# Gate/up norms: eight square tiles folded to two on GpSimd, their sum on TensorE one tile later, and the factor spread inside the fourth tile

## The chip, the cores and the metric

One NeuronCore of a Trainium2 chip runs the whole program. The metric is device time in microseconds (us), the median of several runs. One execution was also taken by the hardware profiler; all rows below come from it. Engine names are those of the profile: PE is TensorE (PEld its weight loads), DVE is VectorE, ACT is ScalarE, POOL is GpSimd, SP is the engine that issues the transfers.

## The reference

Two layers of an encoder over 576 positions (512 of a prompt and 64 of a sample), model width 1024, feed-forward width 2816. Each layer begins and ends with a half-step feed-forward block, so there are four of them:

```python
def rmsnorm(x, g):
    xf = x.astype(jnp.float32)
    y = xf * lax.rsqrt(jnp.mean(xf * xf, axis=-1, keepdims=True) + EPS)
    return (y * g.astype(jnp.float32)).astype(x.dtype)

def ffn_half(x, g, wg, wu, wd):
    h = rmsnorm(x, g)
    return x + 0.5 * ((jax.nn.silu(h @ wg) * (h @ wu)) @ wd)

def layer(h, ...):
    h = ffn_half(h, n1, w1g, w1u, w1d)
    z = rmsnorm(h, nm) @ w_in
    m, st = token_mix(z, ...)
    h = h + m @ w_out
    h = ffn_half(h, n2, w2g, w2u, w2d)
```

## The kernel before, in words

The activations lie transposed in `h`: 128 partitions by 8 tiles by 576 positions. Every matrix product is made of three matmuls of a high and a low part (high*high, high*low, low*high), so every operand is split: ACT rounds the high part, DVE or POOL subtracts it for the low part. The positions are taken in two halves of 288.

Each of the four feed-forward blocks has a gate/up stage. It begins with four plain tiles and goes on with "sets" of seven products, which save one product in eight by working on sums of blocks (`A11, A12, S1, S2, S3, S4, A22`). I call the stretch from the first plain tile to the first set an opening; there are four, one in each block. In an opening:

- PE (`plain_tile` and what follows it) computes up tile 0, up tile 1, then sums the squares of `h` over the model width (`sum_thirds` with the eight tiles `squares`, three column groups each), then gate tile 0, then spreads the norm's factor to all partitions (`spread_thirds`), then gate tile 1. Then comes the first set, `one_set(1, 0)`. Its product A12 waits until ACT has copied the spread factor (`rms_spread`), its product S1 waits for DVE's low part of S1 and for the first scaled gate tile (`g_scaled`), S2 for DVE's low part of S2, and so on. A plain tile waits for its own low parts (`plain_low`).
- ACT (`opening`, then `plain_tiles`) ends the split of `h`, squares the eight tiles (`square`), then makes for each pair p of tiles of `h` an unrounded copy (`full`), the high parts of the gate columns (`plain_chunks`), copies of finished PSUM tiles (`keep_up`), the high parts of the block sums of pair p (`combined_of`), the root (`root`), and the copies of the spread factor (`keep_scale`).
- DVE (`plain_tiles` of the vector block) forms the block sums of pair p from ACT's `full` copies (`even_sum`, `odd_sums`: four short operations, T1, T2, T4, T3), the low parts of the gate columns (`plain_chunk_low`), the low parts of the block sums of two pairs at once (`t_low_of_two`, four operations), the reciprocal of the root (`make_scale`, placed between the work on pairs 0, 1 and that on pairs 2, 3), then the first set's weight sums and low parts (`combine`, `chunk_low`) and the scaled gate tiles.
- POOL (`plain_lows`, then `chunk_lows`) makes one low part of the up columns, passes on counts, and then makes the low parts of A11 and A12 of each set.
- SP loads the next columns of a set once `low_by_pool` says that the buffer is free.

All queues are written out by hand and run in order; semaphores tie them together.

The matmuls of the sum are issued by this loop; each call is two MATMUL records in the profile, so eight tiles by three groups are 48 records:

```python
for m, src in enumerate(parts):
    for g in range(3):
        mm = nc.tensor.matmul(ps[pair][32 * g:32 * g + 32, half, 0:THIRD_T], mean_d[:, 0:32], src[:, g * THIRD_T:(g + 1) * THIRD_T], ...)
```

Of the kernel before, what the change touches and what calls it, by code (L numbers as in the profile page):

```python
# [25 lines left out]
ALU = mybir.AluOpType  # L26
# [7 lines left out]
THIRD_T = NT // 3  # L34
KD = D_MODEL // P
# [70 lines left out]
def seat(p):  # L106
# [2 lines left out]
PRODUCTS = {A11: (B11, ALONE, None), A12: (B21, FIRST, 0), S1: (T1, SECOND, 0), S2: (T2, FIRST, 1),  # L109
            S3: (T3, SECOND, 1), S4: (B22, THIRD, 0), A22: (T4, THIRD, 1)}  # L110
C11, C12, C21, C22, U2, U4, U3, P1 = range(8)


def squared(layer, w):
# [4 lines left out]
def plain_before(layer, w):  # L119

    return 2 * layer + w


def set_number(layer, w, i, b):

    return layer * (2 * SETS) + (w * SETS + b) + 2 * i
# [249 lines left out]
def build(nc, a, outs):  # L376
    ctx = ExitStack()
    with ctx:
# [170 lines left out]
        def sem(name):  # L549
            return ctx.enter_context(nc.semaphore(name))  # L550
# [10 lines left out]

        h_ready, xh_ready, x_ready = sem("h_ready"), sem("xh_ready"), sem("x_ready")
        sq_made, sq_added = sem("sq_made"), sem("sq_added")
        sum_done, root_done, rms_ready = sem("sum_done"), sem("root_done"), sem("rms_ready")
        g_scaled, silu_done, prod_ready = sem("g_scaled"), sem("silu_done"), sem("prod_ready")
        set_in = [sem(f"set_in{b}") for b in range(2)]
# [279 lines left out]
        @block.gpsimd  # L846
        def _(pool):
            pool.sem_inc(low_ready, RAW)
            low_of = lambda s, n: dict(out=wl[s % RING][:, 0:n], in0=raw[s % RAW][:, raw_from(s):raw_from(s) + n],
                                       in1=wh[s % RING][:, 0:n].bitcast(F32), op=ALU.subtract)  # L850

            def low(layer, s, ahead):

                pool.wait_ge(high_ready, layer * SLOTS + ahead + (s + 1))
                if s == KEY_SLOT:
                    high, low = key_columns(wh[s % RING])
                    pool.wait_ge(key_high, layer + 1)
                    nc.gpsimd.tensor_tensor(out=low, in0=raw_keys(s), in1=high.bitcast(F32), op=ALU.subtract).then_inc(key_low, 1)
                    uq = slice(2 * KD * C_ROPE, 2 * KD * C_ROPE + KQ * P)
                    nc.gpsimd.tensor_tensor(out=wl[s % RING][:, uq], in0=raw[s % RAW][:, KD * C_ROPE:KD * C_ROPE + KQ * P],  # L860
                                            in1=wh[s % RING][:, uq].bitcast(F32), op=ALU.subtract).then_inc(low_ready, 1)
                    return
                nc.gpsimd.tensor_tensor(**low_of(s, slot_size(s))).then_inc(low_ready, 1)  # L863

            def chunk_lows(q, b):

                for j in (A11, A12):
                    pool.wait_ge(chunk_high, 7 * q + (j + 1))
                    nc.gpsimd.tensor_tensor(out=cl[:, j], in0=set_raw[b][:, :, int(j == A12), 0:P], in1=ch[:, j].bitcast(F32),  # L869
                                            op=ALU.subtract).then_inc(low_by_pool, 1)  # L870

            def plain_lows(layer, w, b):

                q = set_number(layer, w, 0, b)

                for n in range(2):
                    if b == 0 and n == 0:

                        pool.wait_ge(plain_low, 3 * plain_before(layer, w) + 1)
                        pool.sem_inc(low_by_pool, 1)  # L880
                        continue
                    if b == 1:
                        pool.wait_ge(plain_low, 3 * plain_before(layer, w) + n + 2)
                        pool.wait_ge(low_by_pool, 2 * q + n)
                        pool.sem_inc(low_by_pool, 1)
                        continue
                    pool.wait_ge(chunk_high, 7 * q + (3, 7)[n])
                    js = slice(4 * b + 2 * n, 4 * b + 2 * n + 2)
                    src = set_raw[b][:, :, :, n * P:(n + 1) * P].rearrange("p q e c -> p e q c")
                    nc.gpsimd.tensor_tensor(out=cl[:, js], in0=src, in1=ch[:, js].bitcast(F32), op=ALU.subtract).then_inc(low_by_pool, 1)  # L890

            def ffn(layer, w, d):
                for b in range(2):
                    plain_lows(layer, w, b)
                with pool.Fori(1, MP) as i:
                    for b in range(2):
                        chunk_lows(set_number(layer, w, i, b), b)
                pool.wait_ge(low_ready, layer * SLOTS + (d + RAW + DOWN_SLOTS))

            for layer in range(DEPTH):  # L900
                ffn(layer, 0, F1D)
                for s in range(ZIN, F2D):
                    low(layer, s, 0)
                ffn(layer, 1, F2D)
# [3 lines left out]
        def _(act):  # L908
# [266 lines left out]
            def opening(ph, q, count, gain_col, ahead, free):  # L1175

                for p in range(KP):
                    act.wait_ge(h_ready, count + (2 * p + 1))
                    for half, (dst, signal) in enumerate(((tr[p // 2][:, seat(p), 0, B11, :], t_high[0]), (b12[:, p, 0, :], b12_high))):
                        nc.scalar.activation(dst, h[:, 2 * p, half * HALF:(half + 1) * HALF], ACT.Copy, scale=gain_at(gain_col + 2 * p)).then_inc(signal, 1)  # L1180
                    ahead(2 * p)
                    act.wait_ge(h_ready, count + (2 * p + 2))
                    nc.scalar.activation(tr[p // 2][:, seat(p), 0, B21:T1, :], two(h[:, 2 * p + 1, :]), ACT.Copy, scale=gain_at(gain_col + 2 * p + 1)).then_inc(t_high[1], 1)
                    ahead(2 * p + 1)
                    if p in (1, 2):
                        free(p - 1)
                        plain_chunks(q, 0, p - 1)
                for m in range(KD):
                    square(m, count)

            def plain_tiles(layer, w, gain_col, count, free):

                ph, q = 2 * layer + w, set_number(layer, w, 0, 0)
# [9 lines left out]
                def combined_of(p):  # L1203
                    even_combined(ph, p)
                    combined(ph, p)
                full(0)
                full(1)
                free(2)
                plain_chunks(q + 1, 1, 0)
                keep_up(0)  # L1210
                combined_of(0)
                free(3)
                plain_chunks(q + 1, 1, 1)
                combined_of(1)
                root(ph, ps[3][0:96, 0, 0:THIRD_T])
                full(2)
                full(3)
                keep_up(1)
                combined_of(2)
                keep_scale(ph, 0, FIRST, 0)  # L1220
                keep_scale(ph, 1, FIRST, 1)
                combined_of(3)
                chunk(q + 2, 0, A11)
                chunk(q + 2, 0, A12)
                for j in (S1, S2):
                    chunk(q + 2, 0, j)
                for j in (S3, S4):
# [184 lines left out]
        def _(pe):  # L1412
# [30 lines left out]
            def gate_up(layer, w, x_count):  # L1443
# [63 lines left out]
                        pe.wait_ge(rms_spread, 2 * ph + 1)  # L1507
                    spread_thirds(part, ALONE, 0)

                def plain_tile(b, n):  # L1510

                    q = set_number(layer, w, 0, b)
                    pe.wait_ge(h_ready, x_count + (5 + 2 * b + n))
# [7 lines left out]
                    order = [(e, p) for p in range(KP) for e in range(2)] if arrival else [(e, p) for e in range(2) for p in range(KP)]  # L1521
                    for at_k, (e, p) in enumerate(order):
                            j = 4 * b + 2 * n + e
                            if arrival:
                                for signal, count in ((t_ready[B21], ph * KP),) if e else ((t_ready[B11], ph * KP), (b12_ready, plain_before(layer, w) * KP)):
                                    pe.wait_ge(signal, count + (p + 1))
# [4 lines left out]
                                                          start=at_k == 0 and k == 0, stop=at_k == KD - 1 and k == 2)  # L1531
                    mm.then_inc(chunk_used, (3, 4)[n])

                plain_tile(0, 0)
                plain_tile(0, 1)
                pe.wait_ge(sq_made, x_count + KD)
                pe.wait_ge(h_ready, x_count + KD)
                sum_thirds(3, 0, squares)
                plain_tile(1, 0)
                pe.wait_ge(root_done, 2 * ph + 2)  # L1540
                pe.wait_ge(left_made, set_number(layer, w, 0, 0) + 2)
                for part in range(2):
                    spread_thirds(part, FIRST, part)
                plain_tile(1, 1)
                one_set(1, 0)
                one_set(1, 1)
                with pe.Fori(2, MP) as i:
# [309 lines left out]
        def _(dve):  # L1857
# [214 lines left out]
            def gate_up(layer, w, base_slot):  # L2072
# [98 lines left out]
                def plain_tiles():  # L2171
# [4 lines left out]
                    dve.sem_inc(out_made, 8)  # L2176
                    for g in (0, 2):
                        for p in (g, g + 1):
                            even_sum(ph, p, count, gain_col, x_even[:, p, :])
                            odd_sums(ph, p, gain_col, (x_odd[:, p, 0, :], x_odd[:, p, 1, :]))  # L2180
                            if g == 0:
                                plain_chunk_low(q + 1, 1, p)
                        for t in (T1, T2, T3, T4):
                            t_low_of_two(ph, g, t)
                        if g == 0:
                            make_scale(ph)
                    dve.wait_ge(chunk_used, 7 * q + 3)
                    dve.wait_ge(chunk_used, 7 * q + 7)
                    combine(q + 2, 0, S1)
# [464 lines left out]
```

## Time and profile before

| | |
|---|---|
| median of 3 runs | 2038.65 us (2037.93 to 2039.77) |
| span of the profiled execution, first to last instruction | 2036.0 us |
| PE busy in it | 2022.3 us (99%) |
| DVE busy | 1656.7 us (81%) |
| ACT busy | 972.7 us (48%) |
| POOL busy | 356.5 us (18%) |
| mean granted TensorE clock | 0.998 |

A row of the timeline has the start and the length in us, the engine, the line of the code, the operation, the tiles written and read, their shapes and the number of instructions that the row merges; in brackets stands the idle time before it and who ended it. Consecutive operations of one engine overlap a little (some 0.1 us), so the price of an operation inside a chain is the distance from its start to the start of the next. A row of the chain of waits has start, length and line, in order of time.

### The profile page before, as it was taken

The page shows a single profiled execution, that of the slowest core. Times are in us where ns is not written, and L with a number is a line of the kernel's source. Part 1 is how long each engine was busy: PE and PEld are TensorE (multiplying, and loading weights), DVE is VectorE, ACT ScalarE, POOL GpSimd, SP SyncE. Part 2 cuts the span into 40 slices and gives each one's busy share as a digit, 9 for nine tenths or more (in the row PEclk, how much of TensorE's full clock was granted, in tenths as well). Part 3 has the DMA queues.
Part 4 walks back from the last instruction along what each step waited for, and adds up shares of the span by engine and source line. Part 5 has one row for each costly group of instructions (what it writes and reads, how often), then busy time and mean ns, then how long its engine had stood idle before and what let it go on. Part 6 is the DMA issues. An engine that isn't in the chain of part 4 may idle for free.

```text
span 2036.0 us, 41020 instructions
## 1 busy us (share of the span) xinstructions
PE 2022.3 (99%) x15467; PEld 1969.6 (97%) x15467; DVE 1656.7 (81%) x2440; ACT 972.7 (48%) x1768; POOL 356.5 (18%) x218
## 2 busy tenths in 40 slices
PE   9999999999999999999999999999999999999998
PEld 8999999999879999999999999999997899999998
DVE  6999998755667999998679999976467589999975
ACT  6544453354646444453364444534546474444532
POOL 1222200032011222200012222002321213222000
PEclk9999999999999999999999999999999999999999
DMA  4323232342112232332223322324221123232321
GB/s 135 96 90 101 85 94 81 90 112 67 35 55 84 84 103 83 102 88 84 78 84 104 103 82 81 113 79 113 76 67 44 56 70 104 90 95 80 104 88 66
DMA packets 234855, 175.41 MB, mean 86 GB/s; under 512 B 35184, under 2 KB 231024, under 8 KB 234736
## 3 DMA queue, kind: packets, MB, share of 16 engines
q1 hardware_dynamic: 232624, 171.68, 28.3%
q10 hardware_dynamic: 2112, 2.10, 0.4%
q8 instruction: 80, 1.31, 0.3%
q14 instruction: 39, 0.32, 0.1%
HBM read 170.14 MB, written 3.62 MB: 85 GB/s over the span
## 4 chain that ended last, share of the span: by engine, by line
PE 98%; DVE 1%; ACT 0%; issue 0%; DVEq 0%; ACTq 0%
PE pair L1474 44%; PE pair L1423 32%; PE pair L1597 9%; PE pair L1530 5%; PE pair L1746 1%; PE pair L1725 1%; PE pair L1737 1%; PE pair L1732 1%; PE pair L1769 1%; PE pair L1754 1%; PE pair L1486 1%; PE pair L1762 0%; PE pair L1715 0%; PE pair L1695 0%; PE pair L1705 0%; PE pair L1688 0%
## 5 line engine op out<-in xcount | busy, mean ns | idle before, releaser
L1474 PE MATMUL pair<-t_parts,chunk_high 128*128 128x288 f32 x4480 | 893.2, 295 | 0.0
L1474 PEld LDWEIGHTS pair<-t_parts,chunk_high 128*128 128x128 f32 x4480 | 719.0, 188 | 0.4 <-DVE chunk_low L2034 0.4
L1474 PE MATMUL pair<-t_parts,chunk_low 128*128 128x288 f32 x2240 | 661.1, 295 | 0.0
L1474 PEld LDWEIGHTS pair<-t_parts,chunk_low 128*128 128x128 f32 x2240 | 420.9, 188 | 0.0
L972 ACT ACTIVATE chunk_high<-chunk_sum 128x512 fp32r<-128x512 f32 x320 | 199.4, 631 | 380.7 <-DVE chunk_sum L2022 184.7
L869 POOL TENSOR_TENSOR chunk_low<-set_raw,chunk_high 128x512 fp32r<-128x512 f32 x160 | 229.4, 1443 | 720.3 <-ACT chunk_high L972 720.3
L863 POOL TENSOR_TENSOR w_low<-raw,w_high 128x1024 fp32r<-128x1024 f32 (+1 forms) x46 | 113.9, 2480 | 589.7 <-ACT w_high L920 589.7
L2034 DVE TENSOR_TENSOR chunk_low<-chunk_sum,chunk_high 128x512 fp32r<-128x512 f32 x320 | 207.2, 689 | 7.8
L1423 PE MATMUL pair<-hidden_high,w_high 128*128 128x288 f32 x896 | 192.1, 296 | 0.0
L1423 PE MATMUL pair<-hidden_low,w_high 128*128 128x288 f32 x896 | 191.8, 296 | 0.0
L1423 PE MATMUL pair<-hidden_high,w_low 128*128 128x288 f32 x896 | 191.7, 296 | 0.0
L920 ACT ACTIVATE w_high<-raw 128x896 fp32r<-128x896 f32 (+2 forms) x110 | 108.6, 990 | 97.2 <-PE pair L1597 55.9
L972 ACT ACTIVATE chunk_high<-set_raw 128x512 fp32r<-128x512 f32 x240 | 145.7, 620 | 0.0
L1423 PEld LDWEIGHTS pair<-hidden_low,w_high 128*128 128x128 f32 x896 | 144.5, 189 | 0.0
L1423 PEld LDWEIGHTS pair<-hidden_high,w_high 128*128 128x128 f32 x896 | 144.3, 189 | 0.0
L1423 PEld LDWEIGHTS pair<-hidden_high,w_low 128*128 128x128 f32 x896 | 144.3, 189 | 0.0
L1423 PE MATMUL pair<-x_high,w_high 128*128 128x288 f32 x448 | 97.9, 300 | 0.0
L1423 PE MATMUL pair<-x_high,w_low 128*128 128x288 f32 x448 | 95.9, 296 | 0.0
L1423 PE MATMUL pair<-x_low,w_high 128*128 128x288 f32 x448 | 95.8, 295 | 0.0
L992 ACT ACTIVATE outputs<-outputs 128x576 f32<-128x576 f32 x88 | 59.1, 686 | 75.3 <-DVE outputs L2103 75.1
L1079 ACT ACTIVATE chunk_high<-chunk_sum 128x512 fp32r<-128x512 f32 x64 | 39.1, 633 | 110.7 <-DVE chunk_sum L1942 94.3
L2017 DVE TENSOR_TENSOR chunk_sum<-set_raw 128x512 f32<-128x512 f32 x80 | 81.6, 1020 | 11.5 <-PE pair L1474 11.4
(295 smaller groups left out, 3793.3 us busy)
## 6 DMA issues: line engine op xcount, KB each, us to landing
set_raw<-in_w_up_dram SPq DMA_DIRECT2D x44, 1024.0 KB, 5.3
set_raw<-in_w_gate_dram SPq DMA_DIRECT2D x44, 1024.0 KB, 5.3
raw<-in_w_down_dram SPq DMA_DIRECT2D x64, 448.0 KB, 3.7
down_raw<-in_w_down_dram SPq DMA_DIRECT2D x16, 1024.0 KB, 5.3
raw<-in_w_in_dram SPq DMA_DIRECT2D x20, 512.0 KB, 3.9
raw<-in_w_in_dram SPq DMA_DIRECT2D x16, 256.0 KB, 3.9
raw<-in_w_out_dram SPq DMA_DIRECT2D x8, 512.0 KB, 3.5
raw<-in_w_out_dram SPq DMA_DIRECT2D x16, 256.0 KB, 3.8
```

The lines of the kernel that those rows point to most:

```text
L863: nc.gpsimd.tensor_tensor(**low_of(s, slot_size(s))).then_inc(low_ready, 1)
L869: nc.gpsimd.tensor_tensor(out=cl[:, j], in0=set_raw[b][:, :, int(j == A12), 0:P], in1=ch[:, j].bitcast(F32), op=ALU.subtract).then_inc(low ...
L920: nc.scalar.activation(wh[s % RING][:, 0:n], raw[s % RAW][:, raw_from(s):raw_from(s) + n], ACT.Copy).then_inc(high_ready, 1)
L972: nc.scalar.activation(ch[:, j], src, ACT.Copy).then_inc(chunk_high, 1)
L992: nc.scalar.activation(g, g, ACT.Silu).then_inc(silu_done, 1)
L1079: nc.scalar.activation(ch[:, down_unit(g, j)], src, ACT.Copy).then_inc(d_high, 1)
L1423: mm = nc.tensor.matmul(ps[p][:, half, 0:HALF], w, x[:, half * HALF:(half + 1) * HALF], start=first and k == 0 and q == 0, stop=last and k ...
L1474: mm = nc.tensor.matmul(out, c[:, j, p, :], tr[p // 2][:, seat(p), x, t, :], start=p == 0 and n == 0, stop=p == KP - 1 and n == 2)
L1530: mm = nc.tensor.matmul(ps[2 * b + n][:, half, 0:HALF], c[:, j, p, :], src, start=at_k == 0 and k == 0, stop=at_k == KD - 1 and k == 2)
L1597: mm = nc.tensor.matmul(out, c[:, down_unit(g, j), p, :], block_part(t, p, x), start=p == 0 and k == 0, stop=p == KP - 1 and k == 2)
L2017: ins = nc.vector.tensor_tensor(cf[:, S1], block(b, 0, 1), block(b, 1, 1), ALU.add)
L2034: nc.vector.tensor_tensor(cl[:, j], src, ch[:, j].bitcast(F32), ALU.subtract).then_inc(low_by_dve, 1)
```

## The change

In each of the four openings:

- POOL gets six additions (`fold_squares`, order `FOLD_ORDER`): squares 0+1, 2+3, 4+5, 6+7, each as soon as both are made, then (0)+(2) and (4)+(6), all in place. They stand in POOL's queue ahead of the counts for the gate columns; the last two stand behind its wait for the first low part of the gate columns.
- PE sums `squares[0]` and `squares[4]` alone (6 calls instead of 24), after gate tile 0 instead of before it, into another PSUM place (ALONE, half 1), and waits first for the folds and for ACT's copy of up tile 0 (`left_made`). The factor is spread inside gate tile 1, after six of its eight steps, instead of ahead of it.
- ACT squares tiles 0 to 3 after the first `full`, 4 and 5 after the second, 6 and 7 after the high parts of gate tile 0. `combined_of(1)` moves ahead of the high parts of gate tile 1; both `keep_up` copies move to behind these; the root moves behind the second `keep_up`, and the high parts A11, A12 of the first set follow it; `keep_scale` comes last.
- DVE makes the reciprocal after the sums of pair 2, ahead of those of pair 3, instead of ahead of both.

```diff
+FOLD_ORDER = [(0, 1), (2, 3), (4, 5), (6, 7), (0, 2), (4, 6)]
+FOLDS = len(FOLD_ORDER)
+            def fold_squares(layer, w, pairs):
+                made, folded = updates(layer, (-1, 1)[w]), FOLDS * (2 * layer + w)
+                for into, other in pairs:
+                    n = FOLD_ORDER.index((into, other))
+                    if n < KD // 2:
+                        pool.wait_ge(sq_made, made + other + 1)
+                    else:
+                        pool.wait_ge(sq_folded, folded + n)
+                    nc.gpsimd.tensor_tensor(out=squares[into][:, :], in0=squares[into][:, :], in1=squares[other][:, :], op=ALU.add).then_inc(sq_folded, 1)
             def plain_lows(layer, w, b):
                 q = set_number(layer, w, 0, b)
+                if b:
+                    fold_squares(layer, w, FOLD_ORDER[:KD // 2])
...
                     if b == 1:
+                        if n:
+                            fold_squares(layer, w, FOLD_ORDER[KD // 2:])
                         pool.wait_ge(plain_low, 3 * plain_before(layer, w) + n + 2)
...
-                for m in range(KD):
-                    square(m, count)
...
                 full(0)
+                for m in range(4):
+                    square(m, count)
                 full(1)
+                square(4, count)
+                square(5, count)
                 free(2)
                 plain_chunks(q + 1, 1, 0)
-                keep_up(0)
+                square(6, count)
+                square(7, count)
                 combined_of(0)
+                combined_of(1)
                 free(3)
                 plain_chunks(q + 1, 1, 1)
-                combined_of(1)
-                root(ph, ps[3][0:96, 0, 0:THIRD_T])
+                keep_up(0)
                 full(2)
                 full(3)
                 keep_up(1)
+                root(ph, ps[ALONE][0:96, 1, 0:THIRD_T])
+                chunk(q + 2, 0, A11)
+                chunk(q + 2, 0, A12)
                 combined_of(2)
+                combined_of(3)
                 keep_scale(ph, 0, FIRST, 0)
                 keep_scale(ph, 1, FIRST, 1)
-                combined_of(3)
-                chunk(q + 2, 0, A11)
-                chunk(q + 2, 0, A12)
...
-                def plain_tile(b, n):
+                def plain_tile(b, n, midway=None):
...
+                            if midway is not None and at_k == KP + KP // 2:
+                                midway()
...
+                def sum_squares():
+                    pe.wait_ge(sq_folded, FOLDS * (ph + 1))
+                    pe.wait_ge(left_made, set_number(layer, w, 0, 0) + 1)
+                    sum_thirds(ALONE, 1, [squares[0], squares[4]])
+                def spread():
+                    pe.wait_ge(left_made, set_number(layer, w, 0, 0) + 2)
+                    for part in range(2):
+                        spread_thirds(part, FIRST, part)
                 plain_tile(0, 0)
                 plain_tile(0, 1)
-                pe.wait_ge(sq_made, x_count + KD)
-                pe.wait_ge(h_ready, x_count + KD)
-                sum_thirds(3, 0, squares)
                 plain_tile(1, 0)
-                pe.wait_ge(root_done, 2 * ph + 2)
-                pe.wait_ge(left_made, set_number(layer, w, 0, 0) + 2)
-                for part in range(2):
-                    spread_thirds(part, FIRST, part)
-                plain_tile(1, 1)
+                sum_squares()
+                plain_tile(1, 1, spread)
...
                         for p in (g, g + 1):
+                            if p == 3:
+                                make_scale(ph)
                             even_sum(ph, p, count, gain_col, x_even[:, p, :])
...
-                        if g == 0:
-                            make_scale(ph)
```

## Rows read from the trace of the kernel before

**Rows 1.** The page, chain that ended last, its shares by engine.
```profile
PE 98%; DVE 1%; ACT 0%; issue 0%; DVEq 0%; ACTq 0%
```
**Rows 2.** Chain in order of time (start, us, line), openings 1, 2 and 3.
```profile
33.77 2.73 PE pair L1486 x48
...
647.04 2.73 PE pair L1486 x48
...
656.31 0.98 PE pair L1500 x6
657.29 6.35 PE pair L1530 x48
663.63 11.40 PE pair L1474 x84
...
1034.12 2.73 PE pair L1486 x48
```
**Rows 3.** Timeline of POOL and DVE together, openings 1 and 2: who holds up whom.
```profile
19.75 2.39 POOL L890 TENSOR_TENSOR chunk_low<-set_raw,chunk_high 128x1024 fp32r<-128x1024 f32 x1 [19.30 <-ACT chunk_high L1173]
20.16 2.30 DVE L2345 SCALAR_TENSOR_TENSOR t_parts<-h,gains,t_parts 128x288 fp32r<-128x288 f32 x1
...
659.18 4.30 DVE L2069 TENSOR_TENSOR t_parts<-t_full,t_parts 128x576 fp32r<-128x576 f32 x3 [0.22 <-ACT t_parts L962]
659.67 3.19 POOL L869 TENSOR_TENSOR chunk_low<-set_raw,chunk_high 128x512 fp32r<-128x512 f32 x2 [23.36 <-ACT chunk_high L972]
669.62 1.29 POOL L869 TENSOR_TENSOR chunk_low<-set_raw,chunk_high 128x512 fp32r<-128x512 f32 x1 [6.76 <-ACT chunk_high L972]
```
**Rows 4.** Timeline of ACT: the squares of openings 1 and 3, then opening 2.
```profile
21.09 3.54 ACT L927 ACTIVATE square<-h 128x576 f32<-128x576 f32 x6
...
1023.54 3.54 ACT L927 ACTIVATE square<-h 128x576 f32<-128x576 f32 x6
...
638.32 3.54 ACT L927 ACTIVATE square<-h 128x576 f32<-128x576 f32 x6
...
642.91 0.52 ACT L1196 ACTIVATE x_even<-h,gains 128x288 f32<-128x288 f32 x1
...
645.09 1.05 ACT L1173 ACTIVATE chunk_high<-set_raw 128x1024 fp32r<-128x1024 f32 x1
646.04 0.63 ACT L1201 ACTIVATE outputs<-pair 128x576 f32<-128x576 f32 x1
646.57 0.43 ACT L950 ACTIVATE t_parts<-t_full 128x288 fp32r<-128x288 f32 x1
...
647.72 1.05 ACT L1173 ACTIVATE chunk_high<-set_raw 128x1024 fp32r<-128x1024 f32 x1
...
649.34 0.93 ACT L962 ACTIVATE t_parts<-t_full 128x864 fp32r<-128x864 f32 x1 [0.24 <-DVE t_full L2055]
650.28 1.28 ACT L977 ACT_TABLE_LOAD   x1
651.58 0.42 ACT L977 ACTIVATE sq_tmp<-pair,eps 96x192 f32<-96x192 f32 x1
```
**Rows 5.** Timeline of DVE in opening 2.
```profile
646.17 1.23 DVE L2340 TENSOR_TENSOR chunk_low<-set_raw,chunk_high 128x1024 fp32r<-128x1024 f32 x1 [0.63 <-ACT chunk_high L1173]
647.31 0.51 DVE L2043 SCALAR_TENSOR_TENSOR t_full<-h,gains,x_even 128x288 f32<-128x288 f32 x1
...
650.36 2.76 DVE L2069 TENSOR_TENSOR t_parts<-t_full,t_parts 128x576 fp32r<-128x576 f32 x4
653.04 1.34 DVE L2007 RECIPROCAL sq_tmp<-sq_tmp 96x192 f32<-96x192 f32 x1
...
663.40 0.68 DVE L2017 TENSOR_TENSOR chunk_sum<-set_raw 128x512 f32<-128x512 f32 x1
...
665.59 0.75 DVE L2196 TENSOR_TENSOR outputs<-pair,rms 128x576 f32<-128x576 f32 x1
...
667.64 1.90 DVE L2034 TENSOR_TENSOR chunk_low<-chunk_sum,chunk_high 128x512 fp32r<-128x512 f32 x3
```

More of the change, by code:

```diff
@@ L563, in build @@
         sq_made, sq_added = sem("sq_made"), sem("sq_added")
+        sq_folded = sem("sq_folded")
         sum_done, root_done, rms_ready = sem("sum_done"), sem("root_done"), sem("rms_ready")
```

## Prediction

> **What bounds the kernel now.** I read the page's chain first: 98% of it is PE [rows 1]. Every us taken from PE comes off the time, unless a wait takes its place. Then the chain in order of time around one opening. It has no gap: the sum of the squares at 647.04 for 2.73 us, gate tile 0 from 649.77, the spread at 656.31 for 0.98, gate tile 1 from 657.29 for 6.35, the first set from 663.63 [rows 2]. The next thing to see is how close the other engines follow. A product of a set takes 1.59 us (11.40 us for 84 matmuls, 12 to a product) [rows 2]. S1, the third, is due at 663.63 + 3.19 = 666.82. The scaled gate tile that it waits for is there at 665.59 + 0.75 = 666.34, and S2, due at 668.42, gets its low part at some 667.64 + 0.69 = 668.33 [rows 5]. So PE runs with 0.5 and 0.1 us in hand, and DVE is busy without a pause from 659.18 up to that point [rows 3, 5]. Moving PE forward without moving DVE forward gives nothing. Third, who holds up DVE: a 128x288 operation that costs about 0.5 us elsewhere (0.51) [rows 5] took 2.30 when it met a POOL operation, and ended 0.32 after it [rows 3]. Three low parts that cost 0.67 each (2.76 for four) [rows 5] took 4.30 instead of 2.1 while POOL made two low parts in 3.19 instead of 2.6 [rows 3]. The two engines took turns, one whole operation each: an operation of DVE with both inputs in SBUF and one of POOL don't run together. Each POOL operation in a busy stretch of DVE costs DVE its own length.
>
> **The change part by part.**
>
> *PE, gained.* 36 of 48 records of the sum go: 36 x 2.73/48 = 2.05 us per opening, 8.2 in all [rows 2]. The spread (0.98) stays; cutting gate tile 1 open I price at nothing, at most one more changeover of 0.2 (gate tile 0 took 6.54 behind the sum, against 6.35) [rows 2].
>
> *POOL, added.* Six additions of 128x576. POOL's two sizes cost 1.29 (512 elements) and 2.39 (1024) [rows 3], so 576 lie at 1.29 + 64/512 x 1.10 = 1.43, and 1.28 where it had to wait for its turn (its start is then behind it). That is 8.4 us of POOL per opening, placed where DVE forms block sums; POOL was idle there (23.36 us before the row at 659.67) [rows 3]. POOL alone is no bound. What it takes from DVE is.
>
> *Opening 2, laid end to end.* Prices [rows 4]: a square 0.57 ((642.91-638.32)/8), a `full` 1.09 ((645.09-642.91)/2), gate high parts 0.95, a `keep_up` 0.53, a pair of combined copies 1.15 (647.72-646.57), its second one 0.93, table load and root 1.72. DVE [rows 5]: gate low parts 1.14, the four sums of a pair 1.91 (650.36-647.31-1.14), four low parts 2.7, reciprocal 1.34 (0.08 of it beside the next).
> ACT from 638.32: full, four squares, full, two squares, high parts to 644.9, squares 6 and 7 to 646.1, copies of pair 0 to 647.2. POOL and DVE, taking turns: folds 641.1 to 642.4, to 643.8, 644.1 to 645.5; DVE's low part for gate tile 0, ready to start at 645.0, runs to 646.6 (due 647.04: it just holds); fold 4 to 647.9; T1 of pair 1 to 648.3; fold 5 to 649.6; T2 to 649.9; fold 6 to 651.2; T4, T3 to 651.9, where before they ended at 649.2 (the copy at 649.34 waited for them) [rows 4]. ACT's second copy then runs to 652.9, the high parts of gate tile 1 to 653.8, `keep_up(0)` to 654.4. PE: gate tile 0 from 647.04 to 653.5; the sum waits for `keep_up(0)`: *0.95 lost*. Sum to 655.2, three quarters of gate tile 1 to 660.0. ACT: two fulls, `keep_up(1)` to 657.1, load and root to 658.75. DVE: gate low parts 653.9 to 655.1, four low parts to 657.8, sums of pair 2 to 659.6, reciprocal to 660.9: the spread, due at 660.0, loses *0.95* more. Gate tile 1 ends at 663.55, against 663.64 before: the whole gain is gone here. Then DVE: sums of pair 3 from 660.9, with POOL's A12 low part in between (1.15), to 663.7; ACT's copy; four low parts from 663.7, with a wait of 0.3 for it, to 666.85, where before they ended at 663.40 (the start of what follows) [rows 5]. From there to the scaled tile it is 666.34 - 663.40 = 2.9: 669.6. A12 starts 0.2 late (the factor's copies stand behind the last combined copy), S1 is due at 666.9 and loses *2.7*, S2 *0.4*. Lost 0.95 + 0.95 + 0.2 + 2.7 + 0.4 = 5.2, gained 2.05: **+3.2 us**.
>
> *The other openings.* What differs is how early ACT starts relative to PE: squares to sum is 647.04 - 638.32 = 8.7 us in opening 2, 12.7 in opening 1, 10.6 in opening 3 [rows 2, 4]; opening 4 repeats opening 2. The same ledger for opening 1: folds are over at 34.8, `keep_up(0)` is early, the reciprocal is ready before the spread; what stays is the end: root 1.85 behind the sum, reciprocal, sums of pair 3, four low parts, 2.9 to the scaled tile, all in a line, and POOL's A11 and A12 in it. S1 loses 1.75, S2 0.45: 2.2 - 2.05 = +0.1. Opening 3: **+1.4**. Opening 4: **+3.2**. Sum 0.1 + 3.2 + 1.4 + 3.2 = 7.9 us.
>
> *The waits that were added or moved.* POOL's counts for the gate columns stand behind the folds and DVE's slower low parts, so SP's next load into that buffer goes out about 5 us later (655 against 650); ACT wants it in the set after the first, past 665: hidden, and if it were later than that, it would cost its lateness once an opening. PE's wait for the folds is never the last one (651.2 against 653.5). The sum's new PSUM place asks for `keep_up(0)`, which is.
>
> *Unknown prices.* A fold: 1.28 to 1.6 (the ledger gives +5.2 at 1.2 and +11.2 at 1.6). Whether folds meet DVE as POOL's low parts do: from nothing (+0.5 in all) to as above. Whether the reciprocal, which has one input in SBUF, takes turns with POOL too: no row shows them together; from no (+7.9) to yes (+12.6). I take no, since the rows that wait have two inputs in SBUF. The Trainium skill (SBUF — State Buffer, "Who interferes with whom") says that a VectorE instruction with at most one SBUF input outside the 2-port modes does not contend, but also that single-input fp32 operations such as copies can be in such a mode; by the first +7.9 stays, by the second, if it held for a reciprocal, it would be +12.6. No row here decides it.
>
> **The rivals.**
>
> *Faster: the folds and the short sums don't meet.* If DVE ran undisturbed (POOL's own lows too), each opening would lose only 0.35 at S1 and 0.45 at S2 of its 2.05: -1.27 x 4 = -5.1, 2033.6 us. Against it: both kinds of row show the turns [rows 3].
>
> *No change: POOL's low parts take turns, the folds slip into DVE's pauses.* Then each opening loses what opening 1 does: +0.1 x 4 = +0.5, 2039.1. For it: in opening 1 the folds do hardly any harm; against it: in openings 2 and 4 ACT, DVE and POOL have 4 us less.
>
> *Slower by more: the reciprocal takes turns.* In each opening POOL makes A11 and A12 right beside it; one more low part (1.15 to 1.3) is then in the line to S1: 7.9 + 4.7 = 12.6, 2051.3. It decides from the point where POOL holds the place when the root is done.
>
> *It does not do what it says.* If six calls cost more than a quarter of 24 (a floor for starting and ending the group, up to 1 us), gate tile 1 ends later, but S1 still waits for DVE; the cost would be under 0.3 per opening.
>
> **How the numbers follow.** The profiled span is 2036.0, the median 2038.65; 2.65 lie outside the span, unchanged. 2038.65 + 7.9 = 2046.6 us (span 2043.9). Chances: forecast, +4.1 to +11: 0.60. Reciprocal takes turns, about +12.6: 0.15. Folds harmless or half as bad, 0 to +4: 0.18. No turns, -5: 0.07. The range leaves out the last and the far end of the third and of the second: 2038.5 to 2053. A change under 0.2% (4.1 us) can't be told from none: faster 0.07, same 0.18, slower 0.75.
>
> **What would show it.** In the trace after: six POOL additions of 1.3 to 1.5 us in each opening; T1, T2 and T4 of pair 1 in openings 2 and 4 stretched to 1.4 to 1.8 each; the sum at 12 records and 0.7 us, starting 0.9 late in openings 2 and 4; a gap of PE ahead of S1 of 1.7 to 2.7 us, released by DVE's scaled gate tile, in all four; the set from A22 on in step again. I am wrong if the short sums keep 0.5 us beside the folds, or if S1 starts without a gap.

## The result, and the profile after

| | before | after |
|---|---|---|
| median | 2037.93 us (2037.10 to 2039.77, 5 runs) | 2050.81 us (2050.38 to 2051.75, 5 runs) |
| span of the profiled execution | 2036.0 us | 2049.0 us |
| mean granted TensorE clock in it | 0.998 | 0.995 |

The changed kernel is slower: +12.9 us, ratio 1.0063 with a 95% interval of 1.0052 to 1.0074. The forecast was +7.9 (2046.6 us from the earlier median of 2038.65; 2045.8 from the one in this table). The direction and the waits that were forecast hold, and 5 us are missing from the sum: +12.9 lies above the forecast's own band of +4.1 to +11.

The page's chain of the changed kernel, its shares by engine, answers [rows 1]; under it are the longest waits of PE (who waited for whom: us in total, times, longest):

```profile
PE 91%; DVE 5%; ACT 2%; issue 1%; DMA 1%; ACTq 0%; DVEq 0%; SPq 0%
```
```profile
PE pair L1497 <- DVE chunk_low L2065: 9.8, 4, 2.6
PE pair L1509 <- ACT outputs L1218: 2.2, 2, 1.1
...
PE pair L1523 <- DVE sq_tmp L2038: 1.5, 2, 0.8
```

PE was 98% of the chain; now the chain goes through DVE and ACT in each opening. The three waits are new, and they are those that were forecast: S1 in all four openings (L1497), the sum (L1509) and the spread (L1523) in two each. Together they are 13.5 us.

Where it is lost, block by block. In the chain of waits, the first row of L1423 (before) or L1446 (after) behind a gate/up stage is the start of the down stage (start, length inside the looked-at stretch, line). Before:

```profile
273.57 4.53 PE pair L1423 x34
...
887.07 9.07 PE pair L1423 x68
...
1273.96 12.13 PE pair L1423 x91
...
1887.42 16.67 PE pair L1423 x125
```

After:

```profile
275.02 3.06 PE pair L1446 x23
...
892.93 3.20 PE pair L1446 x24
...
1282.51 3.60 PE pair L1446 x27
...
1900.41 3.60 PE pair L1446 x27
```

The changed kernel is late by 1.45, 5.86, 8.55 and 12.99 us at these four points, so the blocks cost 1.45, 4.41, 2.69 and 4.44. The forecast had 0.1, 3.2, 1.4 and 3.2: every one is short by 1.2 to 1.35 us, whatever its own size. That points to a term that was left out of each opening, rather than to a wrong price of one that varies; an experiment below tests it. One caution on opening 1: the clock comes up at a different moment in each profile, so that the end of the up tiles, which no version changes, moves by over 1 us between profiles (32.88 us with four folds, 33.96 with three, both described below). The changed kernel began gate tile 0 at 33.34 where the kernel before had come as far at 33.70, so its opening 1 really cost about 1.8.

Opening 2 of the changed kernel in the timeline (all times stand 1.45 later than in the forecast's ledger, since the first block came out 1.45 late):

```profile
647.67 1.72 POOL L886 TENSOR_TENSOR sq_tmp<-sq_tmp,square 128x576 f32<-128x576 f32 x1 [0.66 <-ACT square L947]
648.02 1.69 DVE L2074 SCALAR_TENSOR_TENSOR t_full<-h,gains,x_even 128x288 f32<-128x288 f32 x1
649.47 1.53 POOL L886 TENSOR_TENSOR square<-square,square 128x576 f32<-128x576 f32 x1
649.81 1.50 DVE L2083 TENSOR_TENSOR t_full<-x_odd,t_full 128x288 f32<-128x288 f32 x1
651.08 1.53 POOL L886 TENSOR_TENSOR square<-square,sq_tmp 128x576 f32<-128x576 f32 x1
651.35 1.57 DVE L2085 TENSOR_TENSOR t_full<-x_odd,t_full 128x288 f32<-128x288 f32 x1
652.84 0.51 DVE L2086 SCALAR_TENSOR_TENSOR t_full<-h,gains,x_odd 128x288 f32<-128x288 f32 x1
655.16 0.63 ACT L1218 ACTIVATE outputs<-pair 128x576 f32<-128x576 f32 x1
655.93 0.85 PE L1509 MATMUL pair<-square,mean_d 128*32 128x192 f32 x12 [1.09 <-ACT outputs L1218]
660.84 2.99 POOL L874 TENSOR_TENSOR chunk_low<-set_raw,chunk_high 128x512 fp32r<-128x512 f32 x2 [8.24 <-ACT chunk_high L992]
661.02 1.34 DVE L2038 RECIPROCAL sq_tmp<-sq_tmp 96x192 f32<-96x192 f32 x1
662.51 1.21 PE L1523 MATMUL pair<-sq_tmp,ident 96*128 96x192 f32 x6 [0.76 <-DVE sq_tmp L2038]
662.80 1.34 DVE L2083 TENSOR_TENSOR t_full<-x_odd,t_full 128x288 f32<-128x288 f32 x1
670.34 0.75 DVE L2227 TENSOR_TENSOR outputs<-pair,rms 128x576 f32<-128x576 f32 x1
671.19 0.50 PE L1497 MATMUL pair<-t_parts,chunk_high 128*128 128x288 f32 x2 [2.64 <-DVE chunk_low L2065]
```

Three short sums of 0.5 us [rows 5] take 1.69, 1.50 and 1.57 and each ends about 0.3 behind a fold, the same picture as [rows 3]. The last fold ends at 652.61 (ledger 651.2 + 1.45 = 652.65), `keep_up(0)` at 655.79 (655.85), the reciprocal at 662.36 (662.35), the scaled gate tile at 671.09 (671.05). The gaps of PE are 1.09, 0.76 and 2.64, where 0.95, 0.95 and 2.7 were forecast. The last row's bracket names `chunk_low`; but that low part ended at 670.42, and PE started 0.10 behind the scaled tile: of two semaphores of one wait the trace named the earlier. So up to the start of S1 the ledger's times of opening 2 are right to 0.1 us; only the split of 1.9 us between the gaps at sum and spread is off by 0.1 to 0.2. What it lacks comes after that.

Windows of the changed kernel behind the gap ahead of S1 (stretch, length, busy and count of PE, PEld, DVE, ACT, POOL, then the granted clock): openings 1 (and the stretch after it), 2, 3, 4.

```profile
54.00:57.50 3.50, 3.50 (x18) 3.50 (x17) 3.40 (x6) 3.48 (x6) 1.07 (x1) 0.52 0.00 0
57.50:65.00 7.50, 7.50 (x58) 7.50 (x58) 7.24 (x11) 3.34 (x7) 1.51 (x2) 1.00 0.48 142
...
672.00:676.00 4.00, 4.00 (x21) 4.00 (x20) 3.90 (x6) 3.97 (x7) 1.28 (x1) 0.58 0.00 0
1062.00:1066.00 4.00, 4.00 (x23) 4.00 (x23) 3.97 (x6) 3.97 (x7) 1.29 (x1) 0.69 0.00 0
1680.00:1684.00 4.00, 4.00 (x24) 4.00 (x24) 4.00 (x6) 3.97 (x7) 1.28 (x1) 0.71 0.00 0
```

PE is busy all the time in them, but with 18 to 24 matmuls where 3.5 to 4 us at full rate hold 26 to 30, and the granted clock is down: behind each of the four gaps it was at its lower level (1.2 GHz of 2.4) for some 3.4 us (4.00 us at a mean of 0.58 is 4.00 x 0.42/0.5 = 3.4 us at half). The Trainium skill (TensorE: Matmul & The Clock Gate, the section on the HAM clock gate) says that the gate follows how busy the engine has lately been and passes half of the pulses in its idle state; the rows agree in that the clock fell behind stretches without work, which here were 1.86 to 2.65 us long.

### The profile page after: what moved, and what is told of

The parts are those of the page before. It is cut to its first block, busy times and chain, and to the rows that moved or that the text cites. A ratio compares the mean times of both kernels' runs of the same rounds, so it can differ in the third digit from the quotient of the medians.

```text
span 2049.0 us, 40756 instructions
## 1 busy us (share of the span) xinstructions
PE 2021.5 (99%) x15323; PEld 1969.8 (96%) x15323; DVE 1667.7 (81%) x2440; ACT 973.7 (48%) x1768; POOL 392.5 (19%) x242
## 4 chain that ended last, share of the span: by engine, by line
PE 91%; DVE 5%; ACT 2%; issue 1%; DMA 1%; ACTq 0%; DVEq 0%; SPq 0%
PE pair L1497 43%; PE pair L1446 32%; PE pair L1628 9%; PE pair L1777 1%; PE pair L1756 1%; DVE t_parts L2100 1%; DVE t_full L2083 1%; PE pair L1768 1%; PE pair L1763 1%; PE pair L1800 1%; PE pair L1785 1%; DVE t_full L2074 1%; ACT square L947 0%; ACT chunk_high L1193 0%; DMA x_tok<-in_x_prompt_dram 0%
## 5 line engine op out<-in xcount | busy, mean ns | idle before, releaser
L1497 PE MATMUL pair<-t_parts,chunk_high 128*128 128x288 f32 x4480 | 898.8, 296 | 9.8 <-DVE chunk_low L2065 9.8
L1497 PEld LDWEIGHTS pair<-t_parts,chunk_high 128*128 128x128 f32 x4480 | 723.6, 189 | 10.6 <-DVE chunk_low L2065 10.6
L1497 PE MATMUL pair<-t_parts,chunk_low 128*128 128x288 f32 x2240 | 663.9, 296 | 0.0
L1497 PEld LDWEIGHTS pair<-t_parts,chunk_low 128*128 128x128 f32 x2240 | 423.6, 189 | 0.0
L1446 PE MATMUL pair<-hidden_high,w_high 128*128 128x288 f32 x896 | 192.0, 296 | 0.0
L1446 PE MATMUL pair<-hidden_high,w_low 128*128 128x288 f32 x896 | 191.8, 296 | 0.0
L1446 PE MATMUL pair<-hidden_low,w_high 128*128 128x288 f32 x896 | 191.7, 295 | 0.0
L1446 PEld LDWEIGHTS pair<-hidden_low,w_high 128*128 128x128 f32 x896 | 144.5, 189 | 0.0
L1446 PEld LDWEIGHTS pair<-hidden_high,w_high 128*128 128x128 f32 x896 | 144.2, 189 | 0.0
L1446 PEld LDWEIGHTS pair<-hidden_high,w_low 128*128 128x128 f32 x896 | 144.2, 189 | 0.0
L1446 PE MATMUL pair<-x_high,w_high 128*128 128x288 f32 x448 | 97.9, 300 | 0.0
L1446 PE MATMUL pair<-x_high,w_low 128*128 128x288 f32 x448 | 95.9, 296 | 0.0
L1446 PE MATMUL pair<-x_low,w_high 128*128 128x288 f32 x448 | 95.8, 296 | 0.0
```

Of the source, the lines that this page charges most:

```text
L1446: mm = nc.tensor.matmul(ps[p][:, half, 0:HALF], w, x[:, half * HALF:(half + 1) * HALF], start=first and k == 0 and q == 0, stop=last and k ...
L1497: mm = nc.tensor.matmul(out, c[:, j, p, :], tr[p // 2][:, seat(p), x, t, :], start=p == 0 and n == 0, stop=p == KP - 1 and n == 2)
```

## The experiments

**The theory and its rivals.** A: the later place of the sum makes DVE's chain late for S1, the folds add to it in openings 2 and 4, and the clock adds about 1 us behind each gap. B: the folds alone are the loss. D: the missing 5 us are later waits inside the sets, and not the clock. Each ratio below is against the kernel before on the same chip: 2037.99 us (20 runs) for the first three experiments and for the three folds, 2038.13 us (27 runs) on another chip for the folds of half the width, the order with no folds and the fourth fold. The trace is of one execution of each kernel, so the falls of the clock are known for that execution and not for the others behind a median.

**The changed kernel with no folds, eight tiles summed in the new place.**

```diff
-                if b:
-                    fold_squares(layer, w, FOLD_ORDER[:KD // 2])
...
-                        if n:
-                            fold_squares(layer, w, FOLD_ORDER[KD // 2:])
...
-                    pe.wait_ge(sq_folded, FOLDS * (ph + 1))
+                    pe.wait_ge(sq_made, x_count + KD)
...
-                    sum_thirds(ALONE, 1, [squares[0], squares[4]])
+                    sum_thirds(ALONE, 1, squares)
```

> The changed kernel without POOL's additions: PE sums all eight square tiles, in the new place behind gate tile 0; all else as changed. Theory A (the sum's later place makes DVE's line from the root to S1 and S2 late, and the folds matter only in openings 2 to 4): PE pays 2.05 us more per opening for the sum, the two gaps at the sum and the spread go, the gap ahead of S1 is 1.7 us in all four openings and S2's 0.45; +2.06 per opening over the kernel before, 8.2 in all, and with a clock that falls behind each gap as in the changed kernel (1.3 each) 13.4: 2046 or 2051 us. Rival B (the folds are what costs): without them the kernel is near the one before, 2039 to 2041 us, and S1 starts without a gap.

Measured: 2048.79 us (2048.42 to 2049.41), ratio 1.0055 (1.0040 to 1.0071). S1 of openings 1 and 2, and the clock behind the gaps of openings 1, 2 and 3:

```profile
55.69 0.50 PE L1492 MATMUL pair<-t_parts,chunk_high 128*128 128x288 f32 x2 [1.82 <-DVE chunk_low L2060]
...
671.33 0.51 PE L1492 MATMUL pair<-t_parts,chunk_high 128*128 128x288 f32 x2 [1.81 <-DVE chunk_low L2060]
```
```profile
56.00:60.00 4.00, 3.87 (x29) 3.63 (x28) 3.90 (x7) 3.77 (x6) 1.14 (x1) 1.00 0.01 4
672.00:676.00 4.00, 4.00 (x20) 3.67 (x20) 3.90 (x6) 3.97 (x7) 1.27 (x1) 0.61 0.00 0
1062.50:1066.50 4.00, 3.87 (x30) 3.65 (x29) 3.90 (x6) 3.97 (x7) 1.29 (x1) 1.00 0.01 4
```

B is refuted. The time lies between the two that A gave (2046 and 2051), and without any fold it is still 10.8 us slower than before: the gap ahead of S1 is 1.8 in every opening, and the gaps ahead of sum and spread are gone. The line root, reciprocal, sums of pair 3, low parts, scaled tile starts at the end of the sum, and the sum ends one plain tile later. The clock fell behind one of the four gaps.

**The same with two square tiles only**, so that the sum is as short as in the changed kernel: PE's gain without its price (`sum_thirds(ALONE, 1, [squares[0], squares[4]])` in the kernel above). It leaves six tiles out of the norm, so the result is wrong.

> The changed kernel without POOL's additions, and PE sums square tiles 0 and 4 alone: the other six are left out of the norm, so this is the change with its folds free of cost. Theory A: PE gains 2.05 us per opening and loses 1.7 at S1 and 0.45 at S2 in each: +0.1 each, +0.3 in all, and +5.5 with the clock's fall behind the gap (2038.3 or 2043.5 us). If a gap of 1.7 us lets no clock fall, the first number. Rival B: the whole gain of 8.2 us appears, 2029.8 us.

Measured: 2042.79 us (2041.27 to 2043.92), ratio 1.0024 (1.0014 to 1.0034). The gaps ahead of S1 are 1.78, 1.77, 1.77 and 1.77. Since the whole line hangs on the end of the sum, shortening the sum moves S1 as far as PE, and the gap stays. The medians differ by 2048.79 - 2042.79 = 6.0 us, where 36 records in four openings should be worth 8.2. The two profiled executions (2048.66 and 2041.76) show why. The clock behind the gaps of openings 1 and 2 of the kernel with two tiles; it fell behind 3 and 4 too:

```profile
53.00:57.00 4.00, 3.87 (x29) 3.63 (x28) 3.90 (x7) 3.89 (x7) 1.27 (x1) 1.00 0.00 0
667.00:671.00 4.00, 4.00 (x20) 4.00 (x20) 3.90 (x6) 3.97 (x7) 1.28 (x1) 0.58 0.00 0
```

Block by block, from the first matmul of each down stage in the timeline (how late against before, in us, less how late one block earlier):

| | 1 | 2 | 3 | 4 |
|---|---|---|---|---|
| eight tiles | 2.77 | 3.40 | 2.40 | 2.22 |
| two tiles | -0.36 | 1.32 | 1.60 | 1.36 |
| difference | 3.13 | 2.08 | 0.80 | 0.86 |
| clock fell with | neither | both | two tiles only | two tiles only |

Where the clock fell in both, the 36 records are worth 2.08, as forecast. Where it fell in the second alone, 1.2 less: that is the price of a fall. In opening 1, 1.18 of the 3.13 lie ahead of the sum, which starts at 40.34 in one and at 39.16 in the other behind the same work: the clock came up some 2 us later there (11 matmuls from 22 to 24 us against 17), so 1.95 are left for the records.

**Twelve idle matmuls between A12 and S1.** They compute nothing that is used; they keep PE at work in the gap.

```diff
+FILL = 12
...
                         mm.then_inc(chunk_used, 1)
+                        if after_plain and j == A12:
+                            for _ in range(FILL):
+                                nc.tensor.matmul(ps[ALONE][:, 1, 0:P], mean_d[:, :], ident[:, :], start=True, stop=True)
```

> The changed kernel with 12 idle matmuls of 128x128 (written to a PSUM place that nobody reads) on PE between the first set's A12 and S1, to fill most of the gap ahead of S1. Nothing waits for them. Theory C (the 5 us that the ledger of the openings doesn't hold are the clock, which falls to 1.2 GHz for 3.4 us behind each gap): S1 starts at the same time, the gap is 0.3 us in opening 1 and some 1.2 in the others, the granted clock stays at 1.00 and the time falls by 4 to 6 us against the changed kernel, to 2045 to 2047. Rival D (the 5 us are later waits in the sets): no change, 2050.8, or more by up to 12 x 0.13 per opening.

Measured: 2046.53 us (2046.24 to 2047.27), ratio 1.0044 (1.0029 to 1.0060): 4.3 us faster than the changed kernel by adding work. The filler itself was longer than expected, 24 records in 2.7 us and not 1.6, so no gap is left, and in opening 1, where the gap was 1.86, S1 starts 0.7 us behind the scaled gate tile. Opening 1, a row of the chain and two of the timeline:

```profile
51.29 2.68 PE pair L1503 x24
...
52.24 0.75 DVE L2231 TENSOR_TENSOR outputs<-pair,rms 128x576 f32<-128x576 f32 x1
53.73 0.51 PE L1498 MATMUL pair<-t_parts,chunk_high 128*128 128x288 f32 x2
```

The chain's starts of the four down stages, and the clock where S1 starts in opening 2:

```profile
273.97 4.13 PE pair L1447 x31
...
890.78 5.33 PE pair L1447 x40
...
1279.31 6.80 PE pair L1447 x51
...
1896.05 8.00 PE pair L1447 x60
```
```profile
669.00:673.00 4.00, 3.87 (x30) 3.51 (x29) 3.90 (x7) 2.57 (x6) 0.00 (x0) 1.00 0.02 4
```

Against before the four points are late by 0.40, 3.71, 5.35 and 8.63, so the blocks cost 0.40, 3.31, 1.64 and 3.28: the forecast's 0.1, 3.2, 1.4 and 3.2 with 0.1 to 0.3 more each. (In opening 1 the agreement hides two things that cancel in part: S1 is 0.7 late by the filler, and the up tiles were done some 0.5 earlier than in the kernel before.) Against the changed kernel each block is 1.05, 1.10, 1.05 and 1.16 better, and this profile has no fall of the clock. D expected no change or a loss, and is refuted. The price of a fall is 1.1 to 1.2 in openings 2 to 4, in opening 1 more than 1.05 by what the filler was too long. It is less than the 1.7 us that 3.4 us at half pace lose: the 0.4 us that the forecast had at S2 shows here as a wait of the weight loads (PEld), and in the changed kernel, with PE at half pace, no such wait shows.

**The changed kernel with folds of half the width**, 288 of 576 columns; it leaves the squares of the other positions unfolded, so their norm is wrong.

```diff
-                    nc.gpsimd.tensor_tensor(out=squares[into][:, :], in0=squares[into][:, :], in1=squares[other][:, :], op=ALU.add).then_inc(sq_folded, 1)
+                    nc.gpsimd.tensor_tensor(out=squares[into][:, 0:HALF], in0=squares[into][:, 0:HALF], in1=squares[other][:, 0:HALF], op=ALU.add).then_inc(sq_folded, 1)
```

> The changed kernel with each fold on the first 288 of its 576 columns only, so that the norm's sum is wrong in the other half of the tokens: the folds and what they hold up on VectorE shrink, all waits and the places of sum and spread stay. Theory (the gap ahead of S1 comes from the later place of the sum and the chain behind it, the folds add only their share): the gaps ahead of S1 fall from 2.07 and 2.64 us to about 1.7 (openings 1 and 3) and 2.0 to 2.7 (2 and 4), the ones ahead of sum and spread in openings 2 and 4 close; the time is about 2044.5 to 2047, depending on whether the clock falls behind each remaining gap. Rival (the folds' turns with VectorE are the whole loss): with half of them gone half the loss goes, and with the nine matmuls less the time is at or below the kernel before, 2038 or less.

Measured: 2043.24 us (2041.35 to 2044.34), ratio 1.0025 (1.0015 to 1.0034); 1.3 below the low end of the range for A. S1 in the four openings, then the clock behind each:

```profile
52.12 0.50 PE L1497 MATMUL pair<-t_parts,chunk_high 128*128 128x288 f32 x2 [1.77 <-DVE chunk_low L2065]
...
666.63 0.82 PE L1497 MATMUL pair<-t_parts,chunk_high 128*128 128x288 f32 x2 [2.54 <-DVE chunk_low L2065]
...
1054.91 0.57 PE L1497 MATMUL pair<-t_parts,chunk_high 128*128 128x288 f32 x2 [1.77 <-DVE chunk_low L2065]
...
1670.49 0.51 PE L1497 MATMUL pair<-t_parts,chunk_high 128*128 128x288 f32 x2 [2.54 <-DVE chunk_low L2065]
```
```profile
52.50:56.50 4.00, 3.87 (x29) 3.64 (x29) 3.90 (x7) 3.83 (x6) 1.20 (x1) 1.00 0.00 0
667.00:671.00 4.00, 4.00 (x23) 4.00 (x23) 3.90 (x7) 3.82 (x6) 1.19 (x1) 0.69 0.00 0
1055.50:1059.50 4.00, 4.00 (x21) 4.00 (x21) 3.90 (x6) 3.97 (x7) 1.29 (x1) 0.61 0.02 4
1671.00:1675.00 4.00, 3.87 (x30) 3.63 (x29) 3.90 (x6) 3.94 (x7) 1.29 (x1) 1.00 0.02 4
```

The gaps ahead of sum and spread are gone, the one ahead of S1 stays. The median is neither at 2038 as B has it, nor in A's range. In the profiled execution, which was one of the shorter (2041.55), the clock fell behind two gaps: one of 1.77 and one of 2.54, and not behind another of each. From the first matmul of each down stage its blocks cost -0.82, 1.94, 1.60 and 0.97. Openings 2 and 4 have the same gap, and differ by 0.97 with the fall; opening 1 is low because its up tiles were done 1.0 us earlier than in the changed kernel (its sum starts at 38.74 against 39.77). How many falls stand behind the median of 2043.24 is not known.

**The sum in its old place, three folds.** From here on the order is mended. Squares 0+1, 2+3 and 4+5 are folded; the five tiles that remain are summed ahead of gate tile 0, as before the change; the spread stays inside gate tile 1.

```diff
-FOLD_ORDER = [(0, 1), (2, 3), (4, 5), (6, 7), (0, 2), (4, 6)]
+FOLD_ORDER = [(0, 1), (2, 3), (4, 5)]
...
+                free(3)
+                plain_chunks(q + 1, 1, 1)
                 square(7, count)
                 combined_of(0)
                 combined_of(1)
-                free(3)
-                plain_chunks(q + 1, 1, 1)
...
-                root(ph, ps[ALONE][0:96, 1, 0:THIRD_T])
+                root(ph, ps[3][0:96, 0, 0:THIRD_T])
...
+                    pe.wait_ge(sq_made, x_count + KD)
                     pe.wait_ge(sq_folded, FOLDS * (ph + 1))
-                    pe.wait_ge(left_made, set_number(layer, w, 0, 0) + 1)
-                    sum_thirds(ALONE, 1, [squares[0], squares[4]])
+                    sum_thirds(3, 0, [squares[m] for m in (0, 2, 4, 6, 7)])
...
+                sum_squares()
                 plain_tile(1, 0)
-                sum_squares()
+                pe.wait_ge(root_done, 2 * ph + 2)
                 plain_tile(1, 1, spread)
```

> A version built from the ledger: only the three folds 0+1, 2+3, 4+5, which meet DVE's pauses; PE sums the five tiles left in the old place, ahead of gate tile 0 and in the old PSUM place; the factor is spread inside gate tile 1 as in the change; ACT makes the high parts of gate tile 1 before square 7. Theory A: PE gains 15 to 18 of 48 records, 1.0 us per opening, and as the sum is early again, no gap opens at S1: -1.0 to -1.1 per opening, -4.2 in all against the kernel before (2033.8 us). Rival B (any POOL addition costs DVE its length on the path): +1 to +4 us against the kernel before.

Measured: 2033.72 us (2032.84 to 2034.28, 11 runs), ratio 0.9979 (0.9970 to 0.9988), the fastest of all. PE has no gap ahead of S1, and the blocks cost -0.65, -0.96, -0.95 and -1.00 in the profile. PEld at the sum of opening 2:

```profile
646.50 0.80 PEld L1509 LDWEIGHTS pair<-square,mean_d 128*32 128x32 f32 x18 [0.33 <-ACT square L947]
```

That 0.33 is a wait of the weight loads for a square; PE's own rows show none there.

**The same order with no folds** (eight tiles, old place), which parts the folds' share from the order's.

> e5's order of work with no folds at all: eight squares summed in the old place, the spread inside gate tile 1 as in e5. It parts the two halves of e5's gain: the folds (nine matmuls less per opening) and the order. Theory (ledger): the order alone is worth 0.3 us, so about 2037.7; the three folds of e5 carry the other 4 us, 1.0 us per opening for nine matmuls. Rival (the gain of e5 comes from moving the spread and the products of gate tile 1): within 1 us of e5, under 2034.7. No gap ahead of S1 and full clock in either.

Measured: 2037.64 us (2036.82 to 2039.20, 11 runs), ratio 0.9998 (0.9989 to 1.0007). No gap in the openings. So the order by itself moves the time by no more than a measurement can tell, and three folds are worth 3.8 to 3.9 us (2037.64 - 2033.72; against each chip's own kernel before, 4.3 - 0.5): 18 records less per opening are 18 x 2.73/48 = 1.02 us [rows 2], 4.1 in all. All of PE's gain arrives, with three POOL additions an opening beside it.

**A fourth fold, squares 6 and 7**, in that order; PE sums tiles 0, 2, 4 and 6.

> e5 with a fourth fold (squares 6 and 7), so that the sum in the old place, ahead of gate tile 0, takes four tiles and not five. It tells what the last fold costs when TensorE waits for it. From e5's rows TensorE has three matmuls less per opening to pay for than there (about 0.4 us less), but in openings 2 and 4 the sum must wait for a fold that can start only when square 7 is made: 1.6 us each. Theory (ledger): 2.5 us less than before, about 2035.5; if the clock falls behind these two waits as it did behind the gaps ahead of S1, another 1 us each, 2037.6. Rival (folds beside the sum are free, fewer matmuls is always better): under e5's 2033.7. The trace should show two gaps of about 1.6 us ahead of the first sum matmul, released by GpSimd.

Measured: 2035.55 us (2034.31 to 2037.87, 11 runs), ratio 0.9990 (0.9981 to 0.9999). The timeline of opening 2, POOL's last fold and PE's sum:

```profile
645.06 1.40 POOL L886 TENSOR_TENSOR sq_tmp<-sq_tmp,square 128x576 f32<-128x576 f32 x1 [1.61 <-POOLq L905]
...
646.61 1.18 PE L1509 MATMUL pair<-square,mean_d 128*32 128x192 f32 x18 [1.67 <-POOL sq_tmp L886]
```

One tile less saves 6 x 2.73/48 = 0.34 an opening, and two openings pay 1.67 for it: -1.4 + 3.3 = +1.9, measured +1.8 against three folds. The profile bears it out by block: against three folds, openings 2 and 4 cost 1.20 and 1.22 more, opening 3 0.33 less. The clock did not fall behind these two gaps of 1.67 in it.

## Why the prediction came out as it did

The direction was right, and so was the mechanism up to S1. The measured time lies in the stated range of 2038.5 to 2053 us, but that is luck in part: it is above the forecast's own band, and the range reached so high only to make room for the reciprocal, which did not do what that case says.

- *PE is the bound and gains 36 records*: right. The sum is 12 records in all four openings.
- *Folds and DVE's sums take turns*: right, in place and size (1.69, 1.50, 1.57 us). The rival without turns (2033.6) is refuted by these rows, the one in which folds slip into pauses (2039.1) by the gaps ahead of sum and spread in openings 2 and 4. Opening 3 shows the same three stretched sums (1.68, 1.50, 1.57).
- *Which opening loses what*: right, as the run without clock falls shows (0.40, 3.31, 1.64, 3.28 against 0.1, 3.2, 1.4, 3.2).
- *The reciprocal takes turns too* (the fourth case, 2051.3): wrong, although its time is the nearest to the measured one. In all four openings the reciprocal took 1.34 us beside POOL's low part, its price of before [rows 5], while the sum of two SBUF inputs that comes second behind it took 1.34 to 1.36 instead of 0.46. Of the two readings of the Trainium skill (SBUF — State Buffer, "Who interferes with whom") the first fits here, that an operation with at most one SBUF input doesn't contend. A total that fits is no proof of a mechanism.
- *The new place of the sum waits for `keep_up(0)`*: right, 1.09 for 0.95.
- *Six calls for a quarter of the price*: nearly. The 12 records took 0.78 us up to the next matmul (39.77 to 40.55 in opening 1) against 2.73/4 = 0.68, so there is no floor of 1 us.
- *The end of the ledger, "S1 is due at 666.9 and loses 2.7, S2 0.4", and then "in step again"*: this is the step that failed. It priced a gap of PE as its idle time alone and put what follows at full pace. Each of the four gaps also brought some 3.4 us of half clock behind it, worth 1.05 to 1.16 us net of the filler, 4.3 in all. The trace of before could not have shown the size, since PE had no gap in an opening there; but a gap ahead of a dense stretch of matmuls should have had a term with bounds of its own. With it the sum is 7.9 + 4.3 = 12.2 against 12.9; the rest, 0.7, lies in 0.1 to 0.3 too little per opening.

Put together from the runs, as an estimate: the shorter sum brings -8.2. Its later place costs some +9.3 (the four blocks of the kernel without folds, 10.8, less 1.2 for one fall and 0.2 for up tiles that ended later). The falls cost +4.3. What is left of 12.9, +7.5, is what the folds hold up, and the ledger had 3.1 + 1.3 + 3.1 for it.

What stays open: when a gap of this size makes the clock fall. In the profiles it did behind all four of the changed kernel (1.86 to 2.65), behind three of the four of 1.77 to 1.78 with two tiles, behind one of four of 1.8 without folds, behind one of two of 2.54 and one of two of 1.77 with half folds, and behind none of 1.67 or 1.09. Length alone doesn't tell it. For the medians this leaves some 1.1 us for each fall more or less, in the kernels with gaps; the kernels with the sum in its old place and up to three folds have none.

## What to carry to other kernels

Ask of a moved step what hangs on its end: the sum one tile later, with nothing else gained, cost 10.8 us (one fall of the clock included), more than the 8.2 that its shortening could bring, because root, reciprocal and a line of low parts stood behind it. When a second engine takes over work in parts, stop at the part that the first engine would have to wait for: three folds gained 3.9 us, the fourth gave 1.8 of it back. And where TensorE is the bound and a forecast opens a gap of some 1.8 us or more in a dense run of matmuls, add the clock to its price, with bounds: here it was nothing to 1.25 us a gap. A block's time in one profile is worth comparing only from a point where both versions have done the same work: opening 1 moved by over 1 us ahead of any change.

## What the runs showed of the hardware

Not expected: a gap of PE of 1.77 to 2.65 us, in a stretch otherwise dense, can be followed by some 3.4 us at half clock, and costs 1.0 to 1.25 us beyond itself; and twelve idle matmuls in the gap (24 records, 2.7 us) take that back (2050.81 to 2046.53). Expected, but now shown: a DVE operation with two inputs in SBUF and a POOL addition take turns whole, and the DVE operation that waited (1.50 to 1.69 us for one of 0.5) ends about 0.3 us behind the addition; a reciprocal with one input keeps its 1.34 us beside a POOL operation; a 128x576 addition on POOL takes 1.44 us undisturbed (1.40 in the run with four folds).
